# Forgetting heads: the keys' cumulative gates come from a DRAM scratch and GpSimd instead of rank-one products on TensorE

## The reference, cut to what matters

```python
log_f = jax.nn.log_sigmoid(f_b + b_forget)          # (B, S, 16 heads)
c = lax.cumsum(log_f, axis=1)
s = jnp.einsum('bqhd,bshd->bhqs', q_blk, k) * scale
s = s + c_blk[..., None] - cT[:, :, None, :]        # + c[query] - c[key]
s = jnp.where(q_pos[:, None] >= k_pos[None, :], s, -jnp.inf)
p = jax.nn.softmax(s, axis=-1)
o = jnp.einsum('bhqs,bshd->bqhd', p, v)
```

## Time and profile before

| | before |
|---|---|
| median of 3 runs | 1645.62 us (1645.12 to 1645.73) |
| profiled execution | 1646.34 us |
| span of the trace in it | 1644.4 us |
| TensorE busy | 1623.0 us, 99% |
| VectorE busy | 1016.5 us, 62% |
| ScalarE busy | 864.4 us, 53% |
| GpSimd busy | 25.3 us, 2% |
| mean granted TensorE clock | 0.996 |

### The profile page before, as it was taken

One profiled execution on the slowest core, in us unless ns is written; L12 is line 12 of the kernel. 1 busy time (PEld: TensorE's weight loads), 2 busy tenths in 40 slices (PEclk: granted clock), 3 DMA queues, 4 the chain that ended last, 5 costly groups with the idle time before them and its releaser, 6 DMA issues.

```text
span 1644.4 us, 28084 instructions
## 1 busy us (share of the span) xinstructions
PE 1623.0 (99%) x11092; PEld 1480.1 (90%) x11092; DVE 1016.5 (62%) x1386; ACT 864.4 (53%) x1218; POOL 25.3 (2%) x51
## 2 busy tenths in 40 slices
PE   9999999999999999999999999999999999999997
PEld 8999978889999999999998888888998888898896
DVE  5556565565676777766674444465666455776556
ACT  6455566455445555545454444354433795655555
POOL 2000010000000000000000000010000000000000
PEclk9999999999999999999999999999999999999999
DMA  8655533646666666666665665565656547555552
GB/s 265 177 163 152 152 115 103 212 148 179 203 193 192 192 188 185 188 192 203 202 215 179 198 206 184 183 185 154 186 174 172 161 146 246 178 184 174 175 192 76
DMA packets 155598, 294.86 MB, mean 179 GB/s; under 512 B 13460, under 2 KB 16200, under 8 KB 154872
## 3 DMA queue, kind: packets, MB, share of 16 engines
q1 hardware_dynamic: 154632, 289.76, 57.6%
q0 software_dynamic: 848, 3.90, 0.7%
q10 hardware_dynamic: 32, 0.01, 0.0%
HBM read 291.53 MB, written 2.10 MB: 179 GB/s over the span
## 4 chain that ended last, share of the span: by engine, by line
PE 95%; DVE 2%; ACT 1%; DMA 1%; issue 0%; POOL 0%; SPq 0%; ACTq 0%; DVEq 0%
PE bank L1943 30%; PE bank L1944 29%; PE bank L1945 29%; PE upper L2105 1%; DMA raw<-in_w_in 1%; PE upper L2123 1%; PE upper L2356 1%; DVE w_lo L1112 0%; PE bank L2144 0%; PE bank L2145 0%; PE bank L2146 0%; PE upper L2400 0%; DVE x_tok L1549 0%; PE upper L2448 0%; PE upper L2483 0%
## 5 line engine op out<-in xcount | busy, mean ns | idle before, releaser
L1112 DVE TENSOR_TENSOR w_lo<-raw,w_hi 128x1024 fp32r<-128x1024 f32 (+2 forms) x548 | 656.7, 1210 | 483.4 <-ACT w_hi L562 479.3
L562 ACT ACTIVATE w_hi<-raw 128x1024 fp32r<-128x1024 f32 (+2 forms) x548 | 566.7, 1047 | 526.3 <-PE bank L1945 512.8
L1943 PE MATMUL bank<-hT_hi,w_hi 128*128 128x256 f32 x2176 | 604.9, 278 | 2.9 <-DVE hT_lo L1187 1.2
L1944 PE MATMUL bank<-hT_lo,w_hi 128*128 128x256 f32 x2176 | 601.9, 277 | 0.0
L1945 PE MATMUL bank<-hT_hi,w_lo 128*128 128x256 f32 x2176 | 601.9, 277 | 0.0
L1943 PEld LDWEIGHTS bank<-hT_hi,w_hi 128*128 128x128 f32 x2176 | 408.9, 188 | 4.8 <-issue 2.7
L1944 PEld LDWEIGHTS bank<-hT_lo,w_hi 128*128 128x128 f32 x2176 | 409.0, 188 | 0.1
L1945 PEld LDWEIGHTS bank<-hT_hi,w_lo 128*128 128x128 f32 x2176 | 408.8, 188 | 0.0
L1943 PE MATMUL bank<-w_hi,hT_hi 128*128 128x512 f32 (+1 forms) x640 | 249.3, 390 | 0.0
L1945 PE MATMUL bank<-w_hi,hT_lo 128*128 128x512 f32 (+1 forms) x640 | 246.1, 385 | 0.0
L1944 PE MATMUL bank<-w_lo,hT_hi 128*128 128x512 f32 (+1 forms) x640 | 245.9, 384 | 0.0
(11 more groups left out here) (406 smaller groups left out, 1205.2 us busy)
## 6 DMA issues: line engine op xcount, KB each, us to landing
raw<-in_w_in SPq DMA_DIRECT2D x180, 512.0 KB, 4.2
raw<-in_w_up SPq DMA_DIRECT2D x176, 512.0 KB, 4.4
raw<-in_w_down SPq DMA_DIRECT2D x80, 512.0 KB, 4.6
raw<-in_w_out SPq DMA_DIRECT2D x64, 512.0 KB, 4.3
raw<-in_w_xkv SPq DMA_DIRECT2D x16, 512.0 KB, 4.4
raw<-in_w_down SPq DMA_DIRECT2D x16, 256.0 KB, 3.1
raw<-in_w_xq SPq DMA_DIRECT2D x8, 512.0 KB, 3.6
raw<-in_w_xo SPq DMA_DIRECT2D x8, 512.0 KB, 3.8
```

The lines of the kernel that those rows point to most:

```text
L562: act.activation(w_hi[:, s, at:at + n], raw[:, s, 0:n], ACT.Copy).then_inc(hi_ready, 1)
L1112: dve.tensor_tensor(w_lo[:, s, at:at + n], raw[:, s, 0:n], w_hi[:, s, at:at + n].bitcast(F32), ALU.subtract).then_inc(lo_ready, 1)
L1943: pe.matmul(o, l_hi, r_hi, start=start, stop=False, skip_group_check=True)
L1944: pe.matmul(o, l_hi, r_lo, start=False, stop=False, skip_group_check=True)
```

## The change

The rank-one products and what fed them (`eye2`, its making on GpSimd, the four copies in `lf2`, the split of `cT2`) go. The cumulative sums of the keys are made for 16 rows only (`cT`, plain f32). GpSimd stores them in a DRAM tensor `cum`, and for each forgetting pair loads its two rows, spread over all 128 partitions, into `past_row` (one buffer, `past_rows`), and adds the mask `foxm` into `past` (two buffers, `past_gates`, two instructions). DVE's bias then reads `past` in place of `foxm`, and waits for it. `past` lies in the memory of the window heads' keys and values (the odd buffer) and of a spacer (the even one), so `past_gates(9)` waits until the values of pair 7 are done.

```diff
+            def past_rows(p):
+                n = p - NH // 2
+                if n:
+                    pool.wait_ge(past_ready, 2 * n)
+                pool.dma_start(past_row[:, :, :], cum[2 * n:2 * n + 2, :].partition_broadcast(P)).then_inc(row_loaded, 16)
+
+            def past_gates(p):
+                n = p - NH // 2
+                if n == 1:
+                    pool.wait_ge(pv_done, NH // 2)
+                if n >= 2:
+                    pool.wait_ge(biased_done, p - 1)
+                pool.wait_ge(row_loaded, 16 * (n + 1))
+                for lo, hi in ((0, 128), (128, 384)):
+                    pool.tensor_tensor(past[:, p % 2, :, lo:hi], past_row[:, :, 0:hi - lo],
+                                       foxm[:, lo:hi].unsqueeze(1).broadcast_to([P, 2, hi - lo]), ALU.add).then_inc(past_ready, 1)
+
+            pool.wait_ge(f_c, 2)
+            pool.dma_start(cum[:, :], cT[:, :]).then_inc(cum_stored, 16)
+            pool.wait_ge(cum_stored, 16)
+            for p in range(NH // 2, NH // 2 + 4):
+                past_rows(p)
+                past_gates(p)
+            past_rows(NH // 2 + 4)
             pool.wait_ge(swa_rstd, 1)
...
+            for p in range(NH // 2 + 4, PAIRS):
+                past_gates(p)
+                if p + 1 < PAIRS:
+                    past_rows(p + 1)
...
             def bias(p):
+                if p >= NH // 2:
+                    dve.wait_ge(past_ready, 2 * (p - NH // 2 + 1))
...
-                                                           scalar=c8[:, b, h:h + 1], in1=foxm[:, lo:hi], op0=ALU.add, op1=ALU.add)
+                                                           scalar=c8[:, b, h:h + 1], in1=past[:, s, t, lo:hi], op0=ALU.add, op1=ALU.add)
...
-                    for d in range(4):
-                        dve.tensor_tensor(lf2[:, :, 32 * d:32 * d + 16], fm[:, :, :], fa[:, :, :], ALU.subtract).then_inc(lf_ready, 1)
+                    dve.tensor_tensor(lf2[:, :, 0:NH], fm[:, :, :], fa[:, :, :], ALU.subtract).then_inc(lf_ready, 1)
...
-                    dve.tensor_scalar(cT2[:, :], bank[7][:, 0:S], -HD ** 0.5, None, ALU.mult).then_inc(f_c, 1)
-                    dve.wait_ge(f_c, 2)
-                    for rows in (slice(32, 48), slice(96, 112)):
-                        dve.scalar_tensor_tensor(out=cT2[rows, :], in0=bank[7][rows, 0:S], scalar=-HD ** 0.5,
-                                                 in1=cT2[rows, :].bitcast(F32), op0=ALU.mult, op1=ALU.subtract).then_inc(f_c, 1)
+                    dve.tensor_scalar(cT[:, :], bank[7][0:NH, 0:S], -HD ** 0.5, None, ALU.mult).then_inc(f_c, 1)
...
-                pe.matmul(bank[7][:, 0:128], lf2[:, 0, :], tri[:, :], start=True, stop=True)
+                pe.matmul(bank[7][0:NH, 0:128], lf2[:, 0, 0:NH], tri[:, :], start=True, stop=True)
...
-                        ins = pe.matmul(bank[4 + t][:, lo:hi], q, k, start=b == 0, stop=swa, skip_group_check=True)
-                if not swa:
-
-                    for b, (lo, hi) in enumerate(blocks):
-                        for t in range(2):
-                            rows, h = slice(t * HD, (t + 1) * HD), 2 * c + t
-                            ins = pe.matmul(bank[4 + t][:, lo:hi], eye2[rows, h:h + 1].broadcast_to([HD, P]), cT2[rows, 0:hi - lo],
-                                            start=False, stop=True, skip_group_check=True)
+                        ins = pe.matmul(bank[4 + t][:, lo:hi], q, k, start=b == 0, stop=True, skip_group_check=True)
```

More of the change, by code:

```diff
@@ L159, in build @@
         hold = ctx.enter_context(nc.sbuf_tensor("h_place", [P, 2 * KC * S], F32))
-        (work, _, qaT, _, ka2, va, qbT, kbT, vb, eye2, eye_f, distm, foxm, probs, probsT, biased, sink, sink_neg,
-         bf, fz, fm, fa, lf2, c8, cT2, gain_rows, conv_rows, junk, junk_d) = region([
+        (work, _, qaT, _, ka2, va, qbT, kbT, vb, distm, foxm, probs, probsT, biased, sink, sink_neg,
+         bf, fz, fm, fa, lf2, c8, cT, gain_rows, conv_rows, junk, past_row) = region([
              ("work", [P, NB, D], F32), ("sT_place", [P, D], F32), ("qaT", [P, 8, S], F32), ("ka_spacer", [P, 3 * S], F32),
              ("ka2", [P, 2, S], F32), ("va", [P, NB, P], F32), ("qbT", [P, 8, S], F32), ("kbT", [P, 8, S], F32),
-             ("vb", [P, NB, 1024], F32), ("eye2", [P, NH], F32R), ("eye_f", [P, NH], F32), ("distm", [P, 384], F32), ("foxm", [P, 384], F32),
+             ("vb", [P, NB, 1024], F32), ("distm", [P, 384], F32), ("foxm", [P, 384], F32),
              ("probs", [P, 2, 2, 384], F32), ("probsT", [P, 2, 2, 384], F32), ("biased", [P, 2, 2, 384], F32),
@@ L492, in _ @@
                                    pattern=[[-1, 256]], channel_multiplier=1).then_inc(pool_ready, 1)
-            pool.wait_ge(pool_ready, 11)
-            pool.affine_select(out=eye_f[:, :], in_=eye_f[:, :], compare_op=ALU.not_equal, fill=1.0, base=-32,
-                               pattern=[[-1, NH]], channel_multiplier=1).then_inc(pool_ready, 1)
+            pool.wait_ge(pool_ready, 9)
             pool.affine_select(out=distm[:, 128:384], in_=distm[:, 128:384], compare_op=ALU.is_ge, fill=BIG,
                                base=WINDOW - 1 - 128, pattern=[[1, 256]], channel_multiplier=-1).then_inc(pool_ready, 1)
[L500 to L503, removed]
+            def past_rows(p):
[20 more added lines that the diff above has]
+            past_rows(NH // 2 + 4)
             pool.wait_ge(swa_rstd, 1)
@@ L1277, in _ @@
             dve.wait_ge(mm_done, FIRST_PIECE[1])
[L1278 removed]
+            dve.wait_ge(pool_ready, 10)
             dve.wait_ge(consts_loaded, 32)
             dve.tensor_scalar(sink_neg[:, :], sink[:, :], -1.0, None, ALU.mult).then_inc(dve_ready, 1)
[L1281 removed]
             def first_rows(j):
@@ L2078, in forget_sums @@
                 pe.matmul(bank[6][:, 16:32], tri[:, :], lf2[:, 1, 0:16], start=False, stop=True)
-                pe.matmul(bank[7][:, 0:128], lf2[:, 0, :], tri[:, :], start=True, stop=True)
-                pe.matmul(bank[7][:, 128:256], lf2[:, 0, :], ones[:, :], start=True, stop=False)
-                pe.matmul(bank[7][:, 128:256], lf2[:, 1, :], tri[:, :], start=False, stop=True).then_inc(f_cum, 1)
+                pe.matmul(bank[7][0:NH, 0:128], lf2[:, 0, 0:NH], tri[:, :], start=True, stop=True)
+                pe.matmul(bank[7][0:NH, 128:256], lf2[:, 0, 0:NH], ones[:, :], start=True, stop=False)
+                pe.matmul(bank[7][0:NH, 128:256], lf2[:, 1, 0:NH], tri[:, :], start=False, stop=True).then_inc(f_cum, 1)
             def scores(p):
```

23 lines of the change are left out of this document (10 added, 13 removed).

## The result

The changed kernel took 1648.22 us (median of 19 runs, 1646.61 to 1654.95) against 1645.72 us (median of 19, 1643.91 to 1646.68): a ratio of 1.0024 with a 95% interval from 1.0016 to 1.0031. It is 2.5 us slower, outside the range of the prediction. Its profiled execution took 1649.62 us, of which 1647.9 are the span, 3.5 more than the span of before.

What follows compares the result with a forecast made beforehand. TensorE, busy 99% of the span, was taken as the bound. +0.2 at the second transposes, -0.48 for pairs 11 and 12 and 0 for the rest gave -0.3: 1645.3 us for the median, range 1643.4 to 1647.7.

Steps and rivals of the forecast that it cites:

- The delay at the second transposes: TensorE's second transposes of outputs wait 1.0 us for `sT_lo`, using up the 0.72 saved: +0.2 us net.
- What goes: The rank-one products cost TensorE 0.24 us a pair; pairs 8 to 12 save that each, pairs 13 to 15 nothing.
- the late pairs: Pairs 13 to 15: values follow ACT's copy of the probabilities, so saving taken as 0, bounds 0 and 0.16 each.
- Edits costed at nothing: Making `eye2`, copies into `lf2` and steps of `cT2` lie beside projection work of a busy TensorE: 0.
- Additions of 1.6 us: GpSimd's two additions for a forgetting pair, on 256 and 512 values, take 1.6 us together.
- Loads of 4.0 us: Each 256 KB load of a pair's rows into 128 partitions lands 4.0 us after issue.
- step 2: At pair 9 DVE's split and GpSimd's additions collide: 1.23 + 1.6 us, one behind the other, end at 205.6.
- The chain from bias(9): Bias(9), 1.0 us later, delays exps, splits, bias(10) and `sT_lo`; the second transposes wait 1.0 us.
- no saving without GpSimd's delay: Rival: GpSimd done by 204.7, or slack behind bias(9), lets 1.2 to 1.9 us of saving arrive: 1644.2; chance 0.24.
- The stretch of the earlier trace: Lower clock from 274.0 to 277.6 costs 1.7 us; rival that it goes: 1643.6, chance 0.07.
- One stretch more: Rival: another stretch at TensorE's lower clock comes, a new gap lying at 227: 1647.0, chance 0.11.
- GpSimd too late for the norm products: Rival: slow loads delay the products 5.0 us, TensorE idles 1.8 us at the first transposes: 1648.5, chance 0.12.

Runs made afterwards that it cites:

- before: The kernel without the change, as first measured and profiled; 1645.72 us.
- after: The changed kernel, as first measured and profiled; 1648.22 us, ratio 1.0024.
- after_spacer: The changed kernel with 128 unused bytes per partition where `eye2` and `eye_f` lay; 1648.63 us, ratio 1.0016.
- before_shift: The kernel before with `eye2` and `eye_f` moved to the end of the region, so masks and all behind lie as in the changed kernel; 1648.23 us, ratio 1.0013.
- own_past_spacer: own_past with 128 unused bytes per partition where `eye2` and `eye_f` lay; 1645.13 us, ratio 0.9997.
- shift_masks: The kernel before with `eye2` and `eye_f` moved behind `foxm`, so only the masks lie 128 bytes lower; 1646.49 us (one run).
- shift_probs: The kernel before with `eye2` and `eye_f` moved behind `probs`, so masks and `probs` lie 128 bytes lower; 1646.86 us (one run).
- probs_up: The kernel before with 128 free bytes between `foxm` and `probs`, so `probs` and all behind lie higher; 1647.97 us (one run).
- after_again: The changed kernel once more, unaltered, for a second trace; 1648.79 us, ratio 1.0015.
- own_past_max: own_past_spacer with GpSimd's additions started after the negated maxima instead of the bias of the pair two before; 1644.03 us, ratio 0.9990.
- before_again: The kernel before once more, unaltered, for a second trace; 1646.83 us (one run).
- no_wait: The changed kernel with GpSimd's work kept, but the bias adds the mask alone and doesn't wait for GpSimd; 1652.22 us (one run).
- own_past: The changed kernel with `past` in memory of its own, so GpSimd's additions don't wait for pair 7's values; 1646.23 us, ratio 1.0001.

## Why the prediction was wrong, point by point

The path was foreseen: GpSimd's wait for pair 7, bias(9) behind it, the idle time at the second transposes. Two terms failed. The removal of arrays was put at 0 and took 1.2 us in the trace. The delay at the second transposes was put at +0.2 and was +1.46, because the additions and the two splits were priced too low, and a later collision was not priced at all.

- *What goes:* right. 0.24 us at pairs 8 to 11 from scores to transposes; from pair 9 to pair 10 only 0.14 arrive in after (13.96 in place of 14.10 us), and 0.22 in after_spacer (13.88), so the moved arrays take something here too. At the late pairs 0.1 each where 0 was taken, within the bound of 0.16; in the changed kernel pair 14 gives it back, since its maxima are held 1.0 us and the values then wait 0.25.
- *Edits costed at nothing:* here the first step failed. "The making of `eye2` ... go ... 0" weighed the instructions and not the memory they freed. `probs` moved by 128 bytes, and pairs 0 to 8 take 1.2 us longer. That the move does it is shown (before_shift, own_past_spacer, after_spacer, shift_masks, shift_probs, probs_up in the trace; in the median for before_shift alone). I know no row of the profile of before that tells it.
- *Additions of 1.6 us:* 1.97. *Loads of 4.0 us:* 4.2 in the median of the profile. Additions and split took as long together as one behind the other, as step 2 had it: 1.22 + 1.97 = 3.19 us from 205.20 is 208.39, where bias(9) began.
- *The chain from bias(9):* the mechanism was right, the size was not. Counted from the scores of pair 9, bias(9) is 1.72 us late where 1.23 was forecast, bias(10) 2.26 where 1.29 was, the second transposes 1.69 where 0.40 was. Here the second step failed, in three terms. The additions were priced at 1.6 us and took 1.97, which, with 205.5 taken for 205.6, is the 0.5 us at bias(9). "They collide with GpSimd as before ... and keep their 3.2 us": the splits took 3.78, another 0.5 at bias(10). And the prediction stopped counting collisions there, though by its own clock GpSimd ran the norm products until after 220 and then the next additions: these stretched two further splits to 2.05 and 2.11 us, and the second pushed `sT_lo` back by 0.36. It priced being late on GpSimd only by who waits for its results, and nobody waited for these.
- *Sum:* -0.3, with 1.2 for the place, 1.3 for the chain and about 0.2 less for the rest, is +2.0; measured +2.5. Extra stretches at the lower clock would fit what is left, as after_again and after_spacer show one each. That the sum comes so near is in part luck, since the medians of before_shift and after_spacer don't add up like the traces.
- *The rivals:* no saving without GpSimd's delay was right as a condition (own_past_max). The stretch of the earlier trace rows is missing in after and its 1.7 us stand at pair 12, but so it is in before_again: this comes and goes without the change. One stretch more, behind the new idle time, came in after_again and after_spacer. "GpSimd too late for the norm products", nearest in the number (1648.5), did not happen: the first transposes waited for nothing, since the second norm product was done at about 224.4, 1.8 us ahead of them where the forecast had 3.2; the loads took 4.2 us. That its number is near is luck.

## What to carry to other kernels

When work moves to an engine beside which another one was seen to run slower, list what runs beside it at every place where it now falls, not only who waits for its result: in no_wait, where nobody waited for the additions, TensorE lost 4.44 us to them and the late products, more than the 2.07 with the wait. An instruction behind a late wait on an in-order engine delays the unrelated work behind it; give its buffer a place of its own before pricing it. And when a change adds or removes an array, run the kernel once with the layout kept by a spacer, so that code and placement are told apart.

## What the runs showed of the hardware that was not expected

- A step of four values per partition on VectorE was held 5.40 to 5.56 us until a row of six GpSimd instructions ended, and 1.0 us beside two. Where it was held, it ended within 0.03 us of GpSimd's last instruction (227.36 against 227.33 in no_wait, 209.10 against 209.07 in own_past, 258.45 against 258.42 in after). A bias that reads PSUM took 1.38 to 1.39 us beside GpSimd or not. "GPSIMD Engine Reference" of the Trainium skill (Key points) says that GpSimd contends with DVE instructions that have two SBUF inputs or run in a 2-port mode. The bias, with one SBUF tensor, agrees. The long hold of the form with one tensor input, at four values, is more than I drew from it.
- It was not held every time: at pair 10 of after it took 0.21 us beside the norm products. And the splits were stretched (3.78 us for two) without waiting for the end of GpSimd's row. Which of the two happens was not settled.
- Moving `probs` by 128 bytes either way took the spacing of matmuls from 0.113 to 0.118 us in every second interval between pairs, at full clock, 1.2 us in all from pair 0 to pair 8.
- The lower clock took the same time in another form from one execution to the next of one kernel: 3.4 us in two stretches in before, 3.4 us in one in before_again (and in after).
